# Rotated queries transposed before the value projection, and in PSUM bank 7 instead of bank 2

## The reference: one layer for context and latent tokens

```python
h = rms_norm(x, norm_mix) * (1 + sc1) + sh1
proj = h @ w_in
qa, ka, va, ga, lr_f, lr_b, qb, kb, vb = jnp.split(proj, ...)   # 256 256 512 512 16 16 512 128 128
# group A: gated linear attention on qa, ka, va, ga, lr_f, lr_b
# group B: grouped-query attention
qh = rms_norm(qb.reshape(B, S, 8, 64), q_norm)
kh = rms_norm(kb.reshape(B, S, 2, 64), k_norm)
q, k = apply_rope(qh, cos, sin), apply_rope(kh, cos, sin)       # latent tokens only
out = jnp.concatenate([o_gla, o_att], axis=-1) @ w_out
x = x + g1 * out
x = x + g2 * moe_ffn(rms_norm(x, norm_ffn) * (1 + sc2) + sh2)   # top 4 of 32 experts
```

## Time and profile before

| | |
|---|---|
| median of three runs | 2660.65 us |
| profiled execution: its time, and its span | 2665.11 us, 2663.4 us |
| PE busy | 2411.1 us, 91% |
| DVE busy | 1541.4 us, 58% |
| ACT busy | 1338.2 us, 50% |
| POOL busy | 819.3 us, 31% |

### The profile page before, as it was taken

How to read it: one execution, slowest core, us unless ns; L and a number is a source line. 1 busy time by engine, 2 the same in 40 slices (tenths; PEclk the granted TensorE clock), 3 DMA queues, 4 the chain that set the end, 5 groups by cost and what they waited for, 6 DMA issues and landing times.

```text
span 2663.4 us, 55254 instructions
## 1 busy us (share of the span) xinstructions
PE 2411.1 (91%) x19101; PEld 1349.4 (51%) x19102; DVE 1541.4 (58%) x1785; ACT 1338.2 (50%) x1395; POOL 819.3 (31%) x948
## 2 busy tenths in 40 slices
PE   6999978799989939999899998889998999999991
PEld 2555544567765524445455554445544555544550
DVE  2222236566635645981862677999779715165975
ACT  1111144355632235871852667888668615165862
POOL 1222222410003344332343343334334423233422
PEclk9999979899999959999999999999999999999996
DMA  8000043430022246991972878999989926167975
GB/s 315 23 18 18 9 142 133 119 94 0 0 105 96 95 182 223 358 365 32 338 285 80 296 270 294 397 397 395 335 300 398 347 54 206 32 239 268 357 277 197
DMA packets 180310, 538.46 MB, mean 202 GB/s; under 512 B 20736, under 2 KB 37554, under 8 KB 180206
## 3 DMA queue, kind: packets, MB, share of 16 engines
q1 hardware_dynamic: 150620, 487.79, 48.2%
q0 software_dynamic: 26720, 46.85, 7.7%
q10 hardware_dynamic: 2916, 3.14, 0.3%
HBM read 493.11 MB, written 45.20 MB: 202 GB/s over the span
## 4 chain that ended last, share of the span: by engine, by line
PE 47%; DVE 6%; issue 5%; DMA 2%; ACT 2%; ACTq 0%; DVEq 0%; POOL 0%; SPq 0%; POOLq 0%
PE psum L1975 42%; DVE arena L1880 4%; PE psum L1964 2%; PE psum L1959 2%; DMA arena<-in_w_down 1%; ACT arena L1799 1%; PE psum L1953 1%; DVE arena L1928 0%; DVE arena L1894 0%; DMA arena<-expert_inputs,arena 0%; DVE arena L1929 0%; DVE arena L1942 0%; DMA arena<-expert_lists 0%; DVE arena L1884 0%; ACT arena L1815 0%
## 5 line engine op out<-in xcount | busy, mean ns | idle before, releaser
L1975 PE MATMUL psum<-arena 128*64 128x512 bf16 x12528 | 1423.7, 383 | 68.8 <-DVE arena L1884 36.2
L1975 PEld LDWEIGHTS psum<-arena 128*64 128x64 bf16 x12528 | 716.6, 111 | 725.5 <-DVE arena L1880 48.6
L1880 DVE TENSOR_TENSOR arena<-arena 128x2048 bf16<-128x2048 f32 x384 | 862.4, 2286 | 188.3 <-ACT arena L1799 182.1
L1799 ACT ACTIVATE arena<-arena 128x2048 bf16<-128x2048 f32 x384 | 723.3, 1905 | 108.4 <-DVE arena L1880 59.6
L1735 POOL DMA_INDIRECT expert_sums<-arena x90 | 185.9, 2066 | 682.1 <-issue 660.4
L541 PE MATMUL psum<-arena 128*128 128x512 f32 (+2 forms) x864 | 300.6, 506 | 1.1 <-ACT arena L397 1.1
L541 PEld LDWEIGHTS psum<-arena 128*128 128x128 f32 x864 | 151.4, 191 | 134.8 <-issue 130.1
L1884 DVE TENSOR_TENSOR arena<-psum,arena 128x512 bf16<-128x512 f32 x87 | 59.8, 687 | 234.3 <-ACT arena L1809 234.3
L1715 POOL DMA_INDIRECT arena<-expert_inputs,arena x88 | 110.7, 1258 | 207.3 <-issue 129.7
L1805 ACT ACTIVATE arena<-psum 128x1024 bf16<-128x1024 bf16 x87 | 88.5, 1018 | 163.1 <-issue 153.2
L1820 ACT ACTIVATE arena<-psum,arena 128x512 f32<-128x512 f32 x87 | 59.3, 682 | 202.9 <-PE psum L1975 202.9
(11 more groups left out here) (254 smaller groups left out, 2156.0 us busy)
## 6 DMA issues: line engine op xcount, KB each, us to landing
arena<-in_w_gu SPq DMA_DIRECT2D x256, 1024.0 KB, 18.9
arena<-in_w_down SPq DMA_DIRECT2D x128, 1024.0 KB, 15.6
arena<-in_w_ada SPq DMA_DIRECT2D x12, 2048.0 KB, 8.4
arena<-in_x_sample SPq DMA_DIRECT2D x16, 512.0 KB, 3.4
arena<-in_w_in SPq DMA_DIRECT2D x3, 2048.0 KB, 20.1
expert_sums<-arena SPq DMA_DIRECT2D x10, 512.0 KB, 6.4
expert_inputs<-arena SPq DMA_DIRECT2D x10, 512.0 KB, 2.8
x_after_mixing<-arena SPq DMA_DIRECT2D x9, 512.0 KB, 2.6
```

Of the source, the lines that this page charges most:

```text
L1799: nc.scalar.activation(w_hi[p][c], raw[p][c], ACT.Copy).then_inc(sem(f"hi_made{c}"), 1)
L1880: nc.vector.tensor_tensor(w_lo[p][c], raw[p][c], w_hi[p][c], ALU.subtract).then_inc(sem(f"lo_made{c}"), 1)
L1975: last = nc.tensor.matmul(bank(b)[group(g)], parts[part][:, cols], w[:, kk, g * H:(g + 1) * H], start=False, stop=(k == KT - 1 and part == 1))
```

## The change

The transposes of the rotated queries are moved in PE's program from behind those of `qks` to a place between the projections `proj_qk` and `proj_va`, together with their wait for `rotated`. They are written into bank 7 instead of bank 2. So they now also wait for `lrT_kept` of the tile before, the transposes of `qks`, which use bank 7 next, wait for `qaT_kept` of the same tile, and the wait for `qaT_kept` at the top of the tile is gone. On DVE the copy of the transposed queries now stands before the copy of `va`. Nothing that is computed changes.

```diff
--- before.py
+++ after.py
@@ -518,10 +518,10 @@
                         dve.wait_ge(sem("qk_weighted"), 2)
                         nc.vector.tensor_copy(by_head(qr, "r v"), by_head(qw, "v r"))
                         nc.vector.tensor_copy(qr[:, H:H + P], qw[:, H:H + P]).then_inc(sem("rotated"), 1)
+                    wait(dve, sem("qa_transposed"), g + 1)
+                    nc.vector.tensor_copy(qaT[:, :, ds(g * P, P)], r3(bank(7), 4)).then_inc(sem("qaT_kept"), 1)
                     wait(dve, sem("proj_va"), g + 1)
                     nc.vector.tensor_copy(v_all[:, ds(g, 1), :], bank(5).unsqueeze(1)).then_inc(sem("v_kept"), 1)
-                    wait(dve, sem("qa_transposed"), g + 1)
-                    nc.vector.tensor_copy(qaT[:, :, ds(g * P, P)], r3(bank(2), 4)).then_inc(sem("qaT_kept"), 1)
                     wait(dve, sem("ga_sig"), g + 1)
                     nc.vector.tensor_tensor(ga_all[:, ds(g, 1), :], bank(6).unsqueeze(1), sg.unsqueeze(1), ALU.mult).then_inc(sem("ga_kept"), 1)
 
@@ -577,7 +577,6 @@
                 def body(g, b, n, latent):
                     wait(pe, sem("hT_ready"), g + 1)
                     wait(pe, sem("qk_scaled"), g)
-                    wait(pe, sem("qaT_kept"), g)
                     loaded = lambda k: None if latent else pe.wait_ge(sem(f"w_in_in{k}"), 16)
                     loaded(0)
                     project(b, 2, 0, C_QB, H, "proj_qb")
@@ -588,18 +587,19 @@
                     wait(pe, sem("qk_staged"), g)
                     loaded(2)
                     project(b, 4, 0, 0, H, "proj_qk")
+                    wait(pe, sem("rotated"), g + 1)
+                    wait(pe, sem("lrT_kept"), g)
+                    for r in range(4):
+                        last = nc.tensor.transpose(bank(7, P, r * P), qr[:, r * P:(r + 1) * P], ident)
+                    last.then_inc(sem("qa_transposed"), 1)
                     wait(pe, sem("v_kept"), g)
                     loaded(3)
                     project(b, 5, 0, 512, H, "proj_va")
                     wait(pe, sem("qk_staged"), g + 1)
-                    wait(pe, sem("lrT_kept"), g)
+                    wait(pe, sem("qaT_kept"), g + 1)
                     for r in range(4):
                         last = nc.tensor.transpose(bank(7, P, r * P), qks[:, r * P:(r + 1) * P], ident)
                     last.then_inc(sem("qk_transposed"), 1)
-                    wait(pe, sem("rotated"), g + 1)
-                    for r in range(4):
-                        last = nc.tensor.transpose(bank(2, P, r * P), qr[:, r * P:(r + 1) * P], ident)
-                    last.then_inc(sem("qa_transposed"), 1)
                     wait(pe, sem("ga_kept"), g)
                     loaded(4)
                     project(b, 6, 0, 1024, H, "proj_ga")
```

## The result

| | before | changed |
|---|---|---|
| median | 2660.14 us (2657.56 to 2665.11, 4 runs) | 2686.76 us (2684.44 to 2690.47, 4 runs) |
| profiled execution: time and span | 2665.11 and 2663.4 us | 2688.14 and 2686.5 us |

The ratio is 1.0100 with a 95% interval of 1.0085 to 1.0116: 22.6 to 30.9 us slower. The forecast was 2685 us, in a range of 2677 to 2693.

A forecast was written before the change was run, and what follows sets the result against it. PE, never waiting inside the latent-tile stage, was taken to bound the kernel; 20.6 us of waits and restarts plus 3.5 us of clock falls made 24.1 us, for a forecast of 2685 us, range 2677 to 2693.

The forecast's parts named there:

- PE bounds the stage, and nothing behind it gives back: Latent-tile projections: PE never waits, so added waits go straight into the end; the barrier behind returns none.
- The wait of 2.52 us: PE between `proj_qk` and the queries' transposes, waiting for `rotated`: 2.52 us in each of 8 latent tiles, 20.2 us.
- Tile 0 free, restart 0.05 us: Tile 0 has no rotation, so no wait; eight transposes behind a wait take 0.05 us longer, 0.4 us in all.
- The waits around bank 7 cost nothing where `proj_va` covers them: PE's waits for `qaT_kept` and `lrT_kept`: over before PE asks, 0 us.
- The price without cover: PE's wait for `qaT_kept` before the transposes of `qks`, without `proj_va` between: 0.9 us a tile.
- The clock, 2 x 1.74 us: PE's granted clock falls behind two of eight waits, 1.74 us each, 3.5 us in all.
- A fall in every tile: Rival: PE's clock falls behind all eight waits, 34.5 us longer, 2695 us; chance 0.10.
- A chain drawn out by the change itself: Rival: a POOL product comes before the chain to `rotated`, 1.3 us a tile, 10 us more, 2695 us; chance 0.03.
- PE passes the waiting transposes: Rival: PE runs the ready `proj_va` in place of the waiting transposes, time unchanged at 2661 us; chance 0.02.

The follow-up runs named there:

- the second experiment: Changed kernel with the queries' transposes put back behind `proj_va`, still in bank 7, those of `qks` right behind them: 2677.26 us, ratio 1.0055.
- two calls' cover: Changed kernel with the queries' transposes inside `proj_va`, behind two of its eight matmul calls: 2670.0 us, ratio 1.0033.
- with bank 2: Changed kernel with the queries' transposes at the new place but in bank 2, with the old waits for banks 2 and 7: 2686.5 us, ratio 1.0095.
- the wait for the queries only: Changed kernel, its queries' transposes waiting for L515 and no longer L516, which is asked for before the tile's last transposes: 2689.82 us, ratio 1.0098.
- the longer chain: Changed kernel with POOL making its second swapped product twice on latent tiles, the second time behind the first: 2702.83 us, ratio 1.0148.

## Why the prediction was right, and where its sizes were off

**PE bounds the stage, and nothing behind it gives back.** Right: the stage grew by 23.4 us, the span by 23.1 us, and the rest kept its 2307.2 us.

**The wait of 2.52 us.** Right for tiles 2, 4, 6 and 8 (2.50 to 2.52 us), which were the ones read. Too small for the odd tiles: 3.02, 2.83, 2.83 and 2.82. So the term is 21.5 us, not 20.2. The difference could be read before. POOL's rows of tile 1 in the kernel before:

```profile
96.20 1.68 POOL L431 TENSOR_TENSOR arena<-arena 128x512 f32<-128x512 f32 x2 [1.14 <-DVE arena L504]
98.11 2.63 POOL L440 TENSOR_TENSOR arena<-arena 128x320 f32<-128x320 f32 x2 [0.23 <-POOL arena L431]
```

In tile 2 the first pause was 1.00 us and there was none before L440. The loop's body holds two tiles, and only the even kind was read: tile 2 and tile 8. The equal duration of all eight L516 says nothing of when they start. The difference lies in the hand-overs: L504 ended 0.22 us before L431 there (95.70 + 0.28 to 96.20) and 0.08 us before it in tile 2 (130.17 + 0.28 to 130.53). Why they are longer in the odd tiles was not tried.

**Tile 0 free, restart 0.05 us.** Right: no wait in tile 0, and 0.06 us a restart.

**The waits around bank 7 cost nothing where `proj_va` covers them.** Right: PE has no wait for `qaT_kept` in the changed kernel. The price without cover was put at 0.9 us a tile and is 1.4 on average: 12.3 us in nine tiles, from the second experiment.

**The clock, 2 x 1.74 us.** Right in kind, too large in size: one fall of 1.35 us in the profiled execution. The errors of +1.3 and -2.1 us nearly cancel, 23.4 us against a sum of 24.1. That the sum came so near is in part luck. So is the forecast's distance of 1.8 us from the median: the medians are 26.6 us apart, the two profiled executions 23.0 (2688.14 less 2665.11). No trace accounts for the 3.6 us between, though the interval of 22.6 to 30.9 us holds all these numbers.

**The rivals.** A fall in every tile did not come: one in eight with the bank changed or not, two with slightly shorter waits, none behind two calls' cover (waits to 1.2 us), five of eight with waits of 3.4 to 3.9 us. The Trainium skill's page "TensorE: Matmul & The Clock Gate", section "HAM oscillation — how this bites in real kernels", tells of a loop with DMA waits of some 3 to 5 us, in which every burst of matmuls starts at the low clock. This case's traces agree only in part: with waits of 3.4 to 3.9 us five of eight bursts had a stretch at 0.50, two of them from their start, and three had none.

A chain drawn out by the change itself was not seen: DVE waits for POOL before L515 for 15.2 us in the stage now and for 15.4 us before. That PE passes the waiting transposes is out: `proj_va` was ready behind them in all eight tiles and stood still, and its weight loads came only behind those of the transposes (101.84 behind 101.45 in tile 1). The Trainium skill's page "PSUM — Partial Sum Buffer", section "Engine vs sequencer instructions", has matmuls start in program order; the eight waits agree with it.

## What to carry to other kernels

Where one engine is busy without a gap, an instruction that waits for a chain over other engines has one question to answer: how much ready work of the busy engine stands between the chain's start and the wait. Here 10.3 us of chain (from the start of the next tile's transposes at 125.67 to 135.93) had 15.1 us of cover in the old place (to 140.72) and 7.7 in the new (to 133.41), and moving the wait behind 3.4 us of work took the cost away whole. When a loop's body holds several turns, read one of each kind before multiplying.

## What the runs showed of the hardware that was not expected

The hand-over between two engines is not one number, though the instructions are the same. With the bank changed at the old place, PE sat idle for 0.87 us in tile 0, 1.11 us in tile 2 and 1.24 us in tile 3, behind the same copy of 0.69 us. In tile 0 the copy started at 71.29, 0.64 us after the transposes at 70.65, and PE 0.14 us after its end; in tile 2 it was 0.76 us (143.57 less 142.81) and 0.25 us. The tiles differ in the program: in the loop the counts to wait for are held in registers, and this kernel then puts a second wait behind each, for `ident_in`, which is long there. That this is the cause was not tried, and it can't be all of it: in the changed kernel's waits for L516, of the same kind, PE started 0.06 us after the release, and odd and even tiles, alike in this, differ.

Falls of the clock do not follow the number of the waits. Eight waits of 2.35 to 2.86 us brought one, eight that were 0.2 us shorter brought two. Within one execution, though, they nearly kept to the kind of tile with the longer waits. In the changed kernel, with bank 2 and with the wait for the queries only, all four falls lie in odd tiles, behind waits of 2.45 to 2.85 us; of the twelve waits of the even tiles, 2.13 to 2.35 us, none brought one. With the longer chain all four odd tiles fell (3.73 to 3.93 us) and one of the four even ones (3.42 to 3.43). Length and kind of tile go together here, so which of the two decides is not shown, nor how many falls an execution has that was not traced.

A fall can also come after PE has started again. In tile 3 of the changed kernel the clock was at 0.50 from 175.70 us, before PE's start at 176.27. In tile 1 with the longer chain PE started at 103.05 at a granted clock of 1.00, which still held from 103.50 to 104.00, and from 105.00 to 106.00 it was 0.50; PE had been busy since its start.

A gain of 0.2 us a tile can be lost to such falls, so single executions of such kernels should be compared by their waits and not by their spans.
